# Query rotations beside the query products, K/V store behind the query weights, compressed sample scores in column strips

## What is computed

```python
def shared_kv(x, c, pos, p):
    h = modulate(rms_norm(x, p['norm_kv']), shift, scale)
    kv = (h @ p['w_kv']).reshape(bsz, seq, 6, N_KV_HEADS, HEAD_DIM)
    rows = jnp.stack([kv[:, :, 0], kv[:, :, 1], rope(kv[:, :, 2], pos), kv[:, :, 3]], axis=2)
    win_rows = jnp.stack([rope(kv[:, :, 4], pos), kv[:, :, 5]], axis=2)

def nsa_mixer(h, pos, w_qg, w_o, ctx):
    proj = h @ w_qg
    q = proj[..., :N_HEADS * HEAD_DIM].reshape(bsz, nq, N_HEADS, HEAD_DIM)
    gates = jax.nn.sigmoid(proj[..., N_HEADS * HEAD_DIM:]...)
    q_plain = (q * scale).reshape(grp)
    q_rot = (rope(q, pos) * scale).reshape(grp)
    o_cmp, p_cmp = compressed_attention(q_plain, ctx['kc'], ctx['vc'], pos)
    idx = select_blocks(p_cmp, pos, ctx['ks'].shape[2])
    ... selected_attention(q_rot, ...), window_attention(q_rot, ...)
```

## Time and profile before

| what | value |
|---|---|
| runs, median (lowest to highest) | 1248.6 us (1240.9 to 1249.3) |
| the profiled execution | 1246.66 us, span 1245.0 us |
| TensorE busy | 1112.8 us, 89% of the span |
| VectorE, ScalarE, GpSimd busy | 829.0, 564.4, 260.9 us |
| chain that ended last | PE 76%, DVE 10%, ACT 4%, DMA 3%, issue 3%, SPq 3% |
| mean granted TensorE clock | 0.93 of 2.4 GHz |

### The profile page before, as it was taken

The page is one execution under the profiler, slowest core; times in us unless marked ns, Lnnn a source line. Parts: engine busy times, 40 slices in busy tenths (PEclk is TensorE's granted clock), DMA queues, the critical chain, the costliest instruction groups (busy, mean ns, idle before and its releaser), DMA issues.

```text
span 1245.0 us, 19186 instructions
## 1 busy us (share of the span) xinstructions
PE 1112.8 (89%) x6852; PEld 734.5 (59%) x6852; DVE 829.0 (67%) x1309; ACT 564.4 (45%) x1145; POOL 260.9 (21%) x384
## 2 busy tenths in 40 slices
PE   3599999989859999999699987899998699999995
PEld 0365556555536666666467665545666366666663
DVE  3689887998676777843654356665454767777444
ACT  2411121212566666654462405664445566666542
POOL 1175554672001121100100020002430012121000
PEclk7789998999879999999899976979999899999998
DMA  8859877656313334344412520004894214432341
GB/s 351 325 185 409 339 295 267 243 200 227 133 69 128 143 136 141 126 149 161 160 69 87 189 82 1 1 1 134 282 297 180 107 70 166 171 136 94 140 153 43
DMA packets 52530, 205.01 MB, mean 165 GB/s; under 512 B 7251, under 2 KB 36051, under 8 KB 41811
## 3 DMA queue, kind: packets, MB, share of 16 engines
q1 hardware_dynamic: 49362, 195.40, 43.2%
q0 software_dynamic: 3072, 8.39, 2.2%
HBM read 199.39 MB, written 4.38 MB: 164 GB/s over the span
## 4 chain that ended last, share of the span: by engine, by line
PE 76%; DVE 10%; ACT 4%; DMA 3%; issue 3%; SPq 3%; DVEq 0%; POOL 0%; ACTq 0%; POOLq 0%
PE PS L472 16%; PE PS L471 15%; PE PS L475 14%; PE PS L611 8%; PE PS L484 4%; DVE space L1357 4%; PE PS L839 3%; DVE wk_sb L1357 2%; PE PS L640 2%; PE PS L810 2%; PE PS L495 2%; PE PS L758 2%; PE PS L589 1%; DVE rinv L1361 1%; SPq L372 1%
## 5 line engine op out<-in xcount | busy, mean ns | idle before, releaser
L471 PE MATMUL PS<-space_rounded 128*128 128x320 f32 x1344 | 566.4, 421 | 32.8 <-DVE space L1357 23.9
L472 PE MATMUL PS<-space_rounded,lo 128*128 128x320 bf16 x1344 | 428.3, 319 | 0.0
L475 PE MATMUL PS<-space,ring 128*128 128x320 bf16 x1344 | 403.3, 300 | 0.0
L1357 DVE TENSOR_TENSOR lo<-ring,space_rounded 128x1024 bf16<-128x1024 f32 (+1 forms) x172 | 205.8, 1200 | 226.1 <-ACT space_rounded L930 224.4
L471 PEld LDWEIGHTS PS<-space_rounded 128*128 128x128 f32 x1344 | 255.9, 190 | 100.4 <-DVE space L1357 28.9
L930 ACT ACTIVATE space_rounded<-ring 128x1024 fp32r<-128x1024 f32 (+1 forms) x172 | 176.7, 1032 | 225.7 <-PE PS L472 221.8
L472 PEld LDWEIGHTS PS<-space_rounded,lo 128*128 128x128 bf16 x1344 | 129.8, 97 | 125.0 <-issue 2.8
L475 PEld LDWEIGHTS PS<-space,ring 128*128 128x128 bf16 x1344 | 135.7, 101 | 0.0
L611 PE MATMUL PS<-space 128*128 128x256 f32 x512 | 116.8, 387 | 0.0
L611 PEld LDWEIGHTS PS<-space 128*128 128x128 f32 x512 | 97.5, 193 | 28.8 <-issue 15.9
L1357 DVE TENSOR_TENSOR space<-space 128x256 f32<-128x256 f32 (+9 forms) x217 | 85.0, 409 | 22.4 <-ACT space L997 16.0
(11 more groups left out here) (206 smaller groups left out, 1438.8 us busy)
## 6 DMA issues: line engine op xcount, KB each, us to landing
ring<-w_mod SPq DMA_DIRECT2D x24, 2048.0 KB, 9.0
ring<-w_up SPq DMA_DIRECT2D x22, 2048.0 KB, 8.0
ring<-w_down SPq DMA_DIRECT2D x16, 1408.0 KB, 6.0
space<-pool_cmp SPq DMA_DIRECT2D x128, 128.0 KB, 2.8
ring<-w_mod_kv SPq DMA_DIRECT2D x4, 2048.0 KB, 10.6
ring<-w_kv SPq DMA_DIRECT2D x3, 2048.0 KB, 9.3
ring<-w_glu SPq DMA_DIRECT2D x2, 2048.0 KB, 10.5
ring<-w_q SPq DMA_DIRECT2D x2, 2048.0 KB, 12.4
```

Of the source, the lines that this page charges most:

```text
L471: pe.matmul(out, wr[:, p % SPLIT, at:at + P], xr[:, k, :], start=start, stop=False)
L472: mm = pe.matmul(out, lo[:, p % SPLIT, at:at + P], xh[:, k, :], start=False, stop=False)
L475: return pe.matmul(out, w, xl[:, k, :], start=False, stop=stop)
L1357: return dve.tensor_tensor(out, a, b, op)
```

## The change

Three things move or change form. The K/V store goes on SP's queue from behind the gate weights to behind chunk k0. The eight query rotations go between the query tiles: two behind the skewed first three tiles, one behind each later tile, the last one behind the last tile; VectorE has only three weight pieces ahead of its first rope and makes one more ahead of each of the first five. And `QBp` gets four parts of 32 columns for each sample, one per K/V head, so that the compressed scores become 32 matmuls with 32 weight columns, each into its own 32 partitions of the PSUM bank, in place of 16 with 128 columns that accumulate in pairs.

```diff
-        QBp = SC1[:, 0:2048].rearrange("p (e b n) -> p e b n", e=2, b=DB)
+        QBp = SC1[:, 0:1024].rearrange("p (h b n) -> p h b n", h=KVH, b=DB)
@@ SP, loop over the chunks
-                if name == "gate":
+                if name == "k0":
                     sp.wait_ge(S("roped"), 4)
                     sp.wait_ge(S("kv_ev"), 12)
                     sp.dma_start(dram["out_kv"], KV).then_inc(S("out_kv"), 16)
@@ TensorE, dense (behind the skewed loop, and behind each later tile)
+                    for i in range(2):
+                        if beside is not None:
+                            beside(i)
...
+                        if beside is not None and m >= 1:
+                            beside(m - 1)
@@ TensorE
-            dense("q", ["q0", "q1"], KT, hb_kv, 4, (0, 1, 2, 3), "q_ev", split_of(5))
-            for i in range(4, 12):
-                pe.wait_ge(S("q_ev"), i - 3)
-                rotated(i, Qp[:, i - 4, :])
+            def rotated_query(m):
+                pe.wait_ge(S("q_ev"), m + 1)
+                rotated(4 + m, Qp[:, m, :])
+
+            dense("q", ["q0", "q1"], KT, hb_kv, 4, (0, 1, 2, 3), "q_ev", split_of(5), beside=rotated_query)
+            rotated_query(KT - 1)
@@ TensorE, compressed scores
-                for hh in range(2):
-                    mm = pe.matmul(PS[:, 7, NC * b:NC * b + NC], QBp[:, hh, b, :], kcT[:, b, hh, :], start=(hh == 0), stop=(hh == 1))
+                for hd in range(KVH):
+                    mm = pe.matmul(PS[32 * hd:32 * hd + 32, 7, NC * b:NC * b + NC], QBp[:, hd, b, :], kcT[:, b, hd // 2, :], start=True, stop=True)
@@ GpSimd
-            spread(lambda r, hh, hp: QBp[r, hh, :, 64 * hh + 32 * hp:64 * hh + 32 * hp + 32], Qp, "qbp_done")
+            spread(lambda r, hh, hp: QBp[r, 2 * hh + hp, :, :], Qp, "qbp_done")
@@ VectorE
-            low_parts(8)
+            low_parts(3)
             for m in range(KT):
+                if m < KT - 3:
+                    low_parts()
                 dve.wait_ge(S("q_ev"), m + 1)
                 rope(4 + m, Qp[:, m, :], Qr[:, m, :])
```

More of the change, by code:

```diff
@@ L501, in h_ready, with dense @@
                 pe.wait_ge(S("hs"), nth_mod[r])
-            def dense(tag, chunks, kt, src, per, banks, ev, ready, norm=None):
+            def dense(tag, chunks, kt, src, per, banks, ev, ready, norm=None, beside=None):
                 m = 0
@@ L1307, in _ @@
             pool.wait_ge(S("conv_rows0"), 2 * FT)
-            pool.memset(QBp.rearrange("p e b n -> p (e b n)"), 0.0).then_inc(S("qb_zero"), 1)
+            pool.memset(QBp.rearrange("p h b n -> p (h b n)"), 0.0).then_inc(S("qb_zero"), 1)
             pool.memset(QBr.rearrange("p h b n -> p (h b n)"), 0.0).then_inc(S("qb_zero"), 1)
```

## The result

The changed kernel takes 1237.58 us (median of 13 runs, 1230.31 to 1239.16) where the kernel before, on the same chip, takes 1248.6: the ratio is 0.9908, with an interval of 0.9880 to 0.9936. A second comparison gave 1236.22 against 1247.6, a ratio of 0.9921 (0.9893 to 0.9950). The gain is 11.0 and 11.4 us, by the intervals 8 to 15 and 6 to 13. The profiled execution took 1233.77 us, with a span of 1232.1 and a mean granted clock of 0.942; it lies 3.8 us under its median, and that difference will turn out to matter.

A forecast was written before the change was run, and what follows sets the result against it. The prediction took TensorE's matmuls as the bound, busy 1112.8 of 1245.0 us, with time to win in its waits and half clock. Gains of 11.0, 2.32 and 1.55 made 14.9: 1246.66 to 1231.8 us, range 1226 to 1240.

The forecast's parts named there:

- the case of 0.29: Whole kernel: the new time lies within one per cent (12.5 us) of the old, chance 0.29.
- B: Rival, chance 0.17: half clock at query start and scores, 1235 us; ten more us at 0.50 behind, 1240.
- C: Rival, chance 0.08: stalls between query tiles as weight pieces come late, rotations at 0.78; 6 us lost, 1238.
- Gap and clock at the query start, 3.87 us: Ahead of the first query product: TensorE's 2.32 us wait goes, and full clock saves another 1.55.
- Six rotations inside the products, 3.6 us: Between the query tiles: six rotations come before the last query product, at 0.6 us each.
- No stall: Between query tiles: VectorE needs 2.8 us per tile, tightest slack 1.7 us, so TensorE never waits.
- X: End of the last query product, 722.72 in the kernel before; forecast about 722.4 after the change.
- The scores, 2.0 us: Compressed scores: 64 instructions in 16 rounds of four at 0.125 us a round; ends 1.8 and 4.1.
- rival A: Rival, chance 0.12: column strips bring nothing per instruction, 0.064 us each, scores 4.1 us, whole 1234.
- The sum, 14.9 us: K/V product's end to compressed-score read: gains of 11.0, 2.32 and 1.55 us, taken off the whole.
- D: Rival, chance 0.03: five query-tile stalls of 2.3 us, each dropping the clock for 3.1; 19 us, 1251.
- E: Rival, chance 0.02: first query weight chunk q0 still lands last despite the moved store; loses 3.9, 1236.

The follow-up runs named there:

- The store alone: Kernel before with only the K/V store moved behind chunk k0 on SP's queue: 1245.63 us, ratio 0.9993.
- The repeat: The changed kernel run once more, unaltered, in a second comparison against the kernel before: 1236.22 us, ratio 0.9921.
- The spare products: Changed kernel plus thirteen matmuls nobody reads, five behind the first prompt scores, eight behind the importance product: 1228.75 and 1230.4 us, ratios 0.9861 and 0.9852.
- the added VectorE work: Changed kernel plus six further VectorE products ahead of each of the first five rotations: 1242.45 us, ratio 0.9975 to the kernel before.
- the strips alone: Kernel before with only the compressed scores as 32-column matmuls, rotations and store as before: 1244.48 us, ratio 0.9980.
- the one with eight more: Changed kernel with the thirteen unread matmuls plus one more ahead of each prompt job's value products: 1226.88 us, ratio 0.9850 to the kernel before.

## Why the prediction was right, and where it wasn't

The forecast was 1232 us with a range of 1226 to 1240, and a chance of 0.69 for a gain of over 1%. The medians of 1237.58 and 1236.22 lie in the range, in its upper part, with gains of 0.9 and 0.8%: the case of 0.29. They lie there by the room that was left for the rivals B and C; the forecast's own range, 1227 to 1236, is missed by 1.6 and 0.2 us. Its terms were right nearly to the microsecond for the stretch, not for the whole.

- **Gap and clock at the query start, 3.87 us.** The store alone gave 3.91. The next limit was the gate products, as forecast: the first query product follows them without a gap.
- **Six rotations inside the products, 3.6 us.** The query tiles follow each other by 4.05 us in place of 3.51, so 0.54 each and 3.24 in all, a little under the 0.6 taken.
- **No stall.** TensorE never waits there. VectorE waits for it instead, ahead of its fourth to seventh rope, by 0.40, 1.25, 2.53 and 2.51 us, so the slack grows up to the sixth. The first and last of these in VectorE's timeline:

```profile
711.98 0.49 DVE L1364 TENSOR_TENSOR space<-PS,consts_sb 128x320 f32<-128x320 f32 x1 [0.40 <-PE PS L674]
...
724.17 0.49 DVE L1364 TENSOR_TENSOR space<-PS,consts_sb 128x320 f32<-128x320 f32 x1 [2.51 <-PE PS L674]
```

- **Behind X.** GpSimd's copies end at X + 2.59 (forecast 2.6), the read comes at X + 4.72 (forecast 4.7), with VectorE as the last of the three chains.
- **The scores, 2.0 us.** They took 1.09, under the lower end of 1.8. The nearest row was eight instructions in 0.23 us, and a single one of these already takes 0.18, a length that instructions in a row share: in the changed kernel one takes 0.22 and 64 take 1.09. The step cost nothing, since VectorE sets the end. The Trainium skill (TensorE: Matmul & The Clock Gate, Back-to-back issue gap) has an issue cost of about 62 ns for each small matmul without hardware decoding and a floor of about 25 ns otherwise; the 0.017 us measured lie under both, so that its rule doesn't hold for these 64. The 1234 us of rival A fall with the same measurement.
- **The sum, 14.9 us.** The stretch gave 15.3. The sum was taken from the profiled execution of the kernel before, 1246.66; from the median of 1248.6 it gives 1233.7. And the terms that are named for the upper end of the forecast's own range, 1.1 for the rotations and 0.8 for the clock, reach 1233.7 from 1231.8, and not 1236.
- **The step that failed** is the one behind the sum: 14.9 us in the stretch were taken as 14.9 in the whole, since what follows hangs on that read. Its assumption that the next stretch begins at half clock as before held: 23.8 us of it behind the new read and 22.5 behind the old one, with the same wait of 3.63 us. In the first profiled execution the whole nearly held too: 1246.66 - 15.3 + 1.5 (ahead of the stretch) + 0.9 (behind it) = 1233.8. But the later prompt jobs, which the change doesn't touch, differ by several microseconds between executions. The repeat took 102.75 us from the read to the samples where the kernel before took 97.67 in its profiled execution: 5.1 us given back, at a mean clock of 0.77 against 0.80. The prediction had named the place ("the stretch behind it gave the time back, and its clock is the place to look") and priced it mostly the other way: the forecast's own range counted a following stretch at full clock as a gain of up to 4 us, and only rival B, at 0.17, counted ten more us at 0.50 as a loss of 5. The repeat has about ten more than the first execution, and lost 4.8.

What is shown is that the stretch got 15.3 us shorter, by which parts, and that the medians fell by 11.0 and 11.4. That the later half clock takes the rest is not shown. For it speaks the repeat, in which little but the clock differs from the first execution. The spare products, which came out at 1228.75 and 1230.4 us, under the forecast, show that half clock in the prompt jobs costs the changed kernel 7.5 us, not that it costs that kernel more than the one before, which has the same half clock right behind its read and another from 826 to 843 us. Open are also why one execution has the half clock from 817 to 834 us and the next one doesn't, and why the medians of the parts fell by 2 to 6 us less than their stretches. The first comparison's interval just reaches the forecast's gain of 14.9 us, the second's ends at 13, so that part of what is missing may be the scatter of the runs.

Of the rivals, A fell with the strips (0.017 and 0.030 us an instruction), C and D with the trace (no stall) and with the added VectorE work (three stalls of 1.53 us, clock 1.00), E with the store's run. D's 1251 also left out the 1.1 us by which C has the rotations dearer. B was wrong for the place it named first, the query start and the scores, both at full clock; its ten more us of half clock behind came in the repeat and not in the first execution.

## What to carry to other kernels

Time a stretch by its own two ends, and the whole by its median: a change that shortened the chain by 15 us ahead of a part that runs at varying clock showed as 11 here, and one profiled execution need not be like the median: they lay up to 9.7 us apart. When a chain on another engine becomes the last, look at what TensorE does meanwhile: idle time that costs nothing by the chain can cost half clock in the products behind it, and a few products that nobody reads were worth 7.5 us here, though nothing in the kernel before. And what a part of a change is worth depends on the parts beside it: the strips alone saved 5.2 us of the stretch, behind the rotations 3.2, while the store's 3.9 added to both.

## What the runs showed of the hardware

- Small matmuls that fill four groups of 32 columns in turn take 0.017 us an instruction at a clock of 1.00 (64 in 1.09 us) and 0.030 at 0.50 (64 in 1.91), far under what 32 full-width ones take (7.09 us at 0.50).
- Three stalls of TensorE of 1.53 us within 24.5 us left the granted clock at 1.00. With idle stretches of 3.58 and 5.06 us it was 0.50 for 24 us, behind one of 2.55 us for at least the next 9.3 us.
- Thirteen products in those two idle stretches, whose result nothing reads, kept the clock at 1.00 through them and left 10 us at 0.50 in place of 24, in both profiled executions of that kernel; in the one with eight more the clock had fallen ahead of them, at 728 us.
- Two executions of one program differ by 17 us of half clock at one place, and by 4 us the other way just before, with TensorE busy for over 90% of the time ahead of it in both.
